# Attention, plan and experts in one program block, expert 0's weights fetched beside the last attention steps, router logits from the unnormalised residual

## The reference

```python
def encode(x, meta_tokens, layers, ln_final_g):
    h = concatenate([meta, x])
    h = h + mixer(rmsnorm(h, p['ln_mix_g']), cos, sin, p)   # windowed attention + gated recurrence, then w_out
    h = h + hier_moe(rmsnorm(h, p['ln_ffn_g']), p)
    return rmsnorm(h, ln_final_g)[:, N_META:]

def hier_moe(u, p):
    grp_logits = uf @ p['w_router_grp'] + p['b_router_grp']      # 4 groups
    grp = argmax(grp_logits)
    exp_logits = uf @ p['w_router_exp'] + p['b_router_exp']      # 32 experts, 8 in each group
    top_v, top_i = lax.top_k(in_grp, TOP_K)                      # the best 2 of the group
    gates = softmax(top_v) * p_grp
    y = expert_dispatch(uf, eid, gates, p['w_exp_gate'], p['w_exp_up'], p['w_exp_down'])

    # for each block of rows of one expert e:
    hid = silu(xb @ w_g[e]) * (xb @ w_u[e])
    return hid @ w_d[e]
```

## Time and profile before

| | us |
|---|---|
| median of 3 runs | 1351.04 |
| lowest and highest of them | 1347.70, 1357.88 |
| the profiled execution | 1343.24 |
| its span in the trace | 1341.2 |
| PE, DVE, ACT, POOL busy | 1203.2, 888.6, 852.0, 281.4 |
| last product of `mix` starts | 602.35 |
| first product of `experts` starts | 654.44 |

### The profile page before, as it was taken

One profiled execution on the slowest core, in us unless ns is written; L12 is line 12 of the kernel. 1 busy time (PEld: TensorE's weight loads), 2 busy tenths in 40 slices (PEclk: granted clock), 3 DMA queues, 4 the chain that ended last, 5 costly groups with the idle time before them and its releaser, 6 DMA issues.

```text
span 1341.2 us, 21877 instructions
## 1 busy us (share of the span) xinstructions
PE 1203.2 (90%) x5939; PEld 1010.3 (75%) x5939; DVE 888.6 (66%) x1111; ACT 852.0 (64%) x1017; POOL 281.4 (21%) x264
## 2 busy tenths in 40 slices
PE   4999999965999999991599999999999999999972
PEld 3998888954778888881378888888888778888851
DVE  5574555343567676653488886565788788888874
ACT  6438888353566665641477775555677677777772
POOL 1000000013022232111013322212232433323320
PEclk9999999955999999995699999999999999999996
DMA  5251110075222224201999988787899999999985
GB/s 188 94 212 40 39 39 16 0 271 156 79 88 83 82 85 132 79 33 35 367 353 388 385 336 296 269 308 265 327 389 380 356 374 377 385 382 380 401 308 234
DMA packets 68710, 302.06 MB, mean 225 GB/s; under 512 B 11883, under 2 KB 22636, under 8 KB 44098
## 3 DMA queue, kind: packets, MB, share of 16 engines
q1 hardware_dynamic: 50850, 262.96, 50.5%
q0 software_dynamic: 17824, 38.66, 11.6%
HBM read 264.57 MB, written 44.43 MB: 230 GB/s over the span
## 4 chain that ended last, share of the span: by engine, by line
PE 35%; DMA 11%; issue 2%; POOL 1%; DVE 1%; POOLq 1%; ACT 1%; ACTq 0%; DVEq 0%; SPq 0%
PE ps_g L1905 11%; PE ps_ey L1942 11%; PE ps_u L1905 10%; DMA h_dram<-y_sb,ix_y 6%; PE ps_ex L1896 2%; DMA ex<-u_dram,ix_x 1%; POOL ix_x L1818 1%; PE ps_eh L1928 1%; DMA late_dram<-y_sb,ix_a 1%; POOLq L1752 1%; DMA z_late<-late_dram,ix_b 1%; DMA out<-cz 0%; DMA raw_d<-in_w_down 0%; DVE g_lo L2067 0%; DVE d_lo L2067 0%
## 5 line engine op out<-in xcount | busy, mean ns | idle before, releaser
L2067 DVE TENSOR_TENSOR d_lo<-raw_d,d_hi 128x2048 fp32r<-128x2048 f32 x62 | 139.5, 2292 | 53.2 <-ACT d_hi L1974 50.8
L2067 DVE TENSOR_TENSOR g_lo<-raw_g,g_hi 128x2048 fp32r<-128x2048 f32 x64 | 143.9, 2289 | 46.3 <-ACT g_hi L1974 46.3
L2067 DVE TENSOR_TENSOR u_lo<-raw_u,u_hi 128x2048 fp32r<-128x2048 f32 x64 | 143.8, 2289 | 10.9 <-ACT u_hi L1974 10.7
L1974 ACT ACTIVATE g_hi<-raw_g 128x2048 fp32r<-128x2048 f32 x64 | 119.2, 1909 | 34.2 <-DMA raw_g<-in_w_gate 25.2
L590 PE MATMUL pj<-h_hi,w_hi 128*128 128x432 f32 x336 | 123.2, 367 | 0.1
L590 PE MATMUL pj<-h_lo,w_hi 128*128 128x432 f32 x336 | 120.5, 359 | 0.0
L590 PE MATMUL pj<-h_hi,w_lo 128*128 128x432 f32 x336 | 120.2, 358 | 0.0
L1974 ACT ACTIVATE u_hi<-raw_u 128x2048 fp32r<-128x2048 f32 x64 | 118.7, 1906 | 0.0
L1905 PE MATMUL ps_g<-g_hi,ex_hi 128*128 128x512 f32 x280 | 112.5, 402 | 5.2 <-DVE ex_lo L2083 5.2
L1974 ACT ACTIVATE d_hi<-raw_d 128x2048 fp32r<-128x2048 f32 x62 | 115.0, 1907 | 0.0
L1905 PE MATMUL ps_u<-u_hi,ex_hi 128*128 128x512 f32 x280 | 113.5, 405 | 0.0
(11 more groups left out here) (292 smaller groups left out, 2696.7 us busy)
## 6 DMA issues: line engine op xcount, KB each, us to landing
raw_g<-in_w_gate SPq DMA_DIRECT2D x64, 1024.0 KB
raw_u<-in_w_up SPq DMA_DIRECT2D x64, 1024.0 KB, 9.8
raw_d<-in_w_down SPq DMA_DIRECT2D x64, 1024.0 KB, 10.7
k_win<-k_dram POOLq DMA_DIRECT2D x20, 384.0 KB, 5.5
w_raw<-in_w_in SPq DMA_DIRECT2D x14, 512.0 KB, 3.9
late_dram<-a_g SPq DMA_DIRECT2D x11, 512.0 KB, 6.5
xh<-in_x SPq DMA_DIRECT2D x10, 512.0 KB, 6.2
h_dram<-xh SPq DMA_DIRECT2D x10, 512.0 KB, 2.7
```

The source lines that it names most:

```text
L1974: act.activation(hi[c][:, :], raw[c][:, :], ACT.Copy).then_inc(hi_done, 1)
L2067: dve.tensor_tensor(lo[c][:, :], raw[c][:, :], hi[c][:, :].bitcast(F32), ALU.subtract).then_inc(lo_done, 1)
```

## The change

1. **One block.** `mix`, `plan` and `experts` write into one `nc.Block()`; the two barriers between them are gone, and each engine walks from one stage into the next. Semaphore waits take the barriers' place: `table_in` before the first use of the table (PE behind `turn_x(1)`, ACT behind `silu_of(0)`, DVE behind the splits of expert 0, SP behind `g_final`, POOL behind `list_y(0)`), `u_out` and `listed` on SP before `lists` is read, `u_out`, `h2_out` and `lists_in` on POOL before the first gather.
2. **Tiles at fixed places.** Since no memory is given back, the tiles of `experts` are laid by address over dead tiles of `mix`: `g_hi`, `g_lo`, `u_hi`, `u_lo` over `wo_hi` and `wo_lo`, the raw gate weights over `q_pre`, the raw up and down weights from the window buffers `k_win` on, and so on. The eight PSUM banks are one tensor `ps`; `square` of the final norm lies in PSUM.
3. **Prefetch.** SP issues expert 0's gate weights in the last attention step (t = 9) and its up and down weights in the next, when the last scores and values are through.
4. **Logits from h.** `turn_u` transposes `xh` itself as soon as `y_read` says that a half is summed. The router is scaled once by `g` (`scale_router`), and `rstd_h` comes in where the bias is added (L1461 of the new program). For the last block, ACT squares behind the two PSUM copies, and DVE writes `u` (`ffn_scale`) behind `hot`; the store of `h2` waits for the sum alone.
5. **Places of single steps.** PE ranks block 8 before its last six output products. The row buffer `xh` is refilled after `turn_u` has read it. POOL takes column 0 of `lists` for the first block without the table. ACT and DVE split all of expert 0's weights at the start, with `split(0, downs)` right behind `x_split(0)`.

```diff
@@ encoder
-            mix(nc, sem, a, (k_pre, v_pre), q_pre, rec, rstd_rec, wo_hi, wo_lo, k_dram, v_tok, v_meta, ident, eps_t, iota_e,
-                counts, h2_dram, u_dram, list_dram)
-        table = top.enter_context(nc.sbuf_tensor("table", [1, MAXBLK * FIELDS], I32))
-        plan(nc, sem, counts, table, table_dram)
-        experts(nc, sem, a, ident, eps_t, table, list_dram, u_dram, h2_dram, late_dram, out)
+            ps = mixer.enter_context(nc.psum_tensor("ps", [P, 8, BANK], F32))
+            block = mixer.enter_context(nc.Block())
+            planned = plan_tensors(nc, mixer, sem, block)
...
@@ mix, sync
+        def prefetch(name, k, c):
+            raw, arrived = raws[name][c], raw_in[name][c]
+            sp.dma_start(raw[:, :], a[name][0].rearrange("(c p k) f -> c p (k f)", p=P, k=k)[c]).then_inc(arrived, 16)
         def outer(b, s):
+            if isinstance(b, int) and b == NB - 1:
+                sp.wait_ge(y_read, 4 * b + 6)
+                sp.dma_start(h2_dram[b * P:b * P + P, :], xh[s][:, :]).then_inc(h2_out, 16)
+                sp.wait_ge(u_done, b + 1)
...
+                if b2 is not None:
+                    sp.wait_ge(u_turned, 2 * b2 + 2)
+                    sp.wait_ge(h2_out, 16 * b2 + 16)
+                    load_x(t, s)
+                if isinstance(t, int) and t == NB - 1:
+                    sp.wait_ge(q_cos_done, NB)
+                    sp.wait_ge(q_swapped, 16 * len(ROTATED) * NB)
+                    for c in range(2):
+                        prefetch("w_gate", 4, c)
+            elif b1 is not None:
+                sp.wait_ge(nmax_done, 2 * NB)
+                sp.wait_ge(av_done, NB + 1)
+                for c in range(2):
+                    prefetch("w_up", 4, c)
+                for c in range(2):
+                    prefetch("w_down", 2, c)
@@ mix, tensor
+            pe.wait_ge(y_read, 4 * b + 5 + i)
...
-                    mm = pe.transpose(ps_t[1 - i][:, k * P:(k + 1) * P], u[:, (4 * i + k) * P:(4 * i + k + 1) * P], ident[:, :])
+                mm = pe.transpose(ps_t[1 - i][:, k * P:(k + 1) * P], xh[s][:, (4 * i + k) * P:(4 * i + k + 1) * P], ident[:, :])
@@ mix, scalar
             if b2 is not None:
                 u_out_of_psum(b2, 1)
+            if last:
+                h2_rms(b2, s)
@@ mix, vector
-                then(dve.tensor_tensor(logits[:, :], ps_x[:, 0:ROUT], rbias[:, :], ALU.add))
+            then(dve.scalar_tensor_tensor(out=logits[:, :], in0=ps_x[:, 0:ROUT], scalar=rstd_h[:, 0:1], in1=rbias[:, :],
+                                          op0=ALU.mult, op1=ALU.add))
...
+            if isinstance(b, int) and b == NB - 1:
+                ffn_scale(b, s)
@@ experts, sync
+        sp.wait_ge(mixed["u_out"], 16 * NB)
+        for s in range(RING):
+            sp.wait_ge(mixed["listed"][s], 16 * NB)
             sp.dma_start(lists[:, :, :], list_dram.rearrange("(p c) o -> p c o", p=P)).then_inc(lists_in, 16)
-            for weights, k, kind in ((a["w_gate"], KG, gates), (a["w_up"], KG, ups), (a["w_down"], KDN, downs)):
-                for c in range(2):
-                    src = weights[0].rearrange("(c p k) f -> c p (k f)", p=P, k=k)[c]
-                    sp.dma_start(kind[0][c][:, :], src).then_inc(kind[3][c], 16)
             sp.dma_start(g_final[:, :], a["ln_final_g"][0].partition_broadcast(P)).then_inc(g_in, 16)
+        sp.wait_ge(table_in, 16)
             load_new(1, a["w_gate"], KG, gates)
@@ experts, scalar
+        act.wait_ge(mixed["y_done"], 4 * NB)
             split(0, gates)
-            x_split(0)
             split(0, ups)
+        act.wait_ge(mixed["u_done"], NB)
+        x_split(0)
+        split(0, downs)
             silu_of(0)
+        act.wait_ge(table_in, 16)
             split_new(1, gates)
             x_split(1)
             split_new(1, ups)
-            split(0, downs)
```

2254 lines of the change are left out of this document (1144 added, 1110 removed).

## The result

The changed kernel took 1337.45 us (median of 20 runs, 1333.3 to 1348.12), the kernel before 1349.02 us (20 runs, 1340.65 to 1357.88) in the same comparison. The ratio of the comparison is 0.9924, with a 95% interval of 0.9905 to 0.9943: 10 us or 0.8% faster (the two medians lie 11.6 us apart). A second comparison gave 0.9928 [0.9900, 0.9955]. The forecast was 15.5 us and 1335.5 us, with a range of 1326 to 1343. Sign and range held. In the profiled executions the gain is smaller: 1334.59 us against 1343.24, with a span of 1332.9 against 1341.2, which is 8.3 us.

A forecast was written before the change was run, and what follows sets the result against it. PE bounds the expert stage; the hole before it is one chain of single steps. Terms 6.2 - 0.9 + 6.8 + 2.1 + 0.8 + 0.5 = 15.5 us, taken from 1351.04, gave 1335.5 us, range 1326 to 1343.

The forecast's parts named there:

- First term: From the last product of `mix` up to the logits' step: that step starts earlier, saving 6.2 us.
- the later of the two branches: Before the logits' step, ACT's square and root end near 607.95, after PE's router product near 607.8.
- Second term: Behind the logits, up to the addresses: DVE writes `u` ahead of four small steps, giving back 0.9 us.
- third term: First barrier, ahead of the plan: the plan starts at once behind `counts`, saving 6.8 us.
- Fourth term: Second barrier, ahead of the lists: table's arrival and barrier no longer hold the lists, saving 2.1 us.
- Fifth term: First gather: 0.8 us saved before POOL's issue, 0.5 us in the gather, taken as 8.2 us instead of 8.66.
- rival A: First gather runs nearly free, about 4 us instead of 8.2, if expert 1's weights come later; 1331.3 us, chance 0.13.
- Prefetch itself: Moving expert 0's six weight transfers beside attention gains 0, since PE waited for the gather.
- The attention steps lose or gain nothing: Attention steps: router's scaling, scaling of `u` and refill of `xh` cost no time; 0 us.
- a stall of PE in the attention steps: Sign in the changed profile that the prediction said would prove it wrong.
- From the first product on: Expert stage from the first gate product: it moves with the gather and itself gains 0.
- Rival D: The shift is given back in the stretch with DMA at 1.00; about 1343 us at worst, chance 0.08.

The follow-up runs named there:

- rlo_late: Changed kernel with POOL's `rec_lo` waiting, from the third step on, until DVE has made `ediff`; 1333.51 us, ratio 0.9901 to the kernel before.
- barriers: Changed kernel cut into three blocks again, so all engines meet between `mix` and `plan` and between `plan` and `experts`; 1342.36 us, ratio 0.9962 to the kernel before.
- best3: Changed kernel plus rlo_late's wait, lists loaded before table, first gather directly from lists, expert 1's weights and `g_final` after it, `ex_lo` before `u_lo`; 1327.07 us.
- stt_before: Kernel before with only the attention steps' logits add exchanged for the change's three-operand form (0.26 us instead of 0.20); 1351.56 us against 1346.40, ratio 1.0042.
- no_prefetch_late: Changed kernel with expert 0's six weight transfers issued behind the lists again and twelve DVE memsets delaying the first scores; 1337.74 us, one profile.
- after_again: The changed kernel itself, measured again as reference for a later group of runs; 1337.67 us, ratio 0.9928 to the kernel before.

## Why the prediction was right or wrong

**First term, 6.2 us: right, 0.6 us short.** The step starts 5.8 us behind the end of the last product instead of 5.2, because the router's product was partly at the low clock (3.05 us; 1.95 in rlo_late, where the stretch gains 6.4 us of the 6.5). The forecast called ACT's root the later of the two branches; in the changed kernel it ends at 614.67 and PE's product decides. The root starts 0.02 us after the load of its function table ends (613.08 + 1.28 = 614.36), so keeping the row, without a further 1.4 us, was right.

**Second term, -0.9 us, and third term, 6.8 us: right.** -0.9 and 6.7 us; barriers confirms the third by putting it back (6.5 us).

**Fourth term, 2.1 us: right in size, wrong in cause.** I called it the second barrier. Of the 2.47 us from the table's load to the lists, the barrier by itself is worth 0.4 us, as barriers shows; the rest, by difference, was the wait for the table to land, which the changed kernel no longer has ahead of the lists.

**Fifth term, 0.8 and 0.5 us: wrong, they are 0.1 and -0.8.** The step that failed is "ACT and DVE now split gate and up weights before the gather lands (9 us of DVE from 619.2 on)". I counted these splits as free, because DVE was idle. They stand beside POOL's copy (1.56 us instead of 0.19) and its issue (2.15 instead of 1.07): 2.4 us of which none was in the sum. best3 takes the splits away from there and has 1.04 us. The gather's size, 8.2 us, was read from one row under other rivals; it is 9.4 us beside 4 MB, counted from an issue that is itself 1.1 us longer, and 4.2 us alone, 1.0 us above the prediction's estimate of 3.2. I had put rival A at 0.13 for the case that expert 1's weights come late by themselves. They did not, since SP issued them at 632.54, ahead of the gather. The mechanism of the rival was right, its condition was not met.

**Prefetch itself, 0: right** in the handover (38.5 us without it, 39.1 with it), but in part by luck: the forecast had neither POOL's 2.4 us beside the early splits nor the 1.7 us by which `ex_lo` is late without them, and the two nearly cancel.

**"The attention steps lose or gain nothing": wrong by 3.4 us** (from the first to the last value product 252.0 us before, 255.4 after). This is the largest miss, and one of the signs that the prediction itself named, a stall of PE in the attention steps (1.09 us in the step shown). I counted the router's scaling, the scaling of `u` and the refill of `xh`, and passed over the logits' own step, since 0.06 us of DVE off the critical path seemed nothing. stt_before shows that in the kernel before this alone makes the three additional long steps; no_prefetch_late shows that it need not, where the steps begin at another distance. It was to be seen: the profile before has one step of 29.2 us with `ediff` at 0.98 us, and `rec_lo` starts within 0.3 us of `ediff` in all others. Rather than ask whether DVE was busy, I should have asked what it holds or is held by.

**The end of mix.** The low clock takes 1.5 us that were in no term, cause open. The ranks of block 8, moved ahead of the last six products, take 21.84 - 21.41 = 0.4 us where I had 0.3. Another 1.6 us are the start of the first step: its value product stands at 328.93 before and 330.54 after, and between 328.8 and 331.8 in the twelve profiles without an added delay, so I take it for scatter.

**From the first product on, 0: not contradicted.** The profiles give 2.3 us of gain there (686.8 us before, 684.5 after, to the end of the span), but the fourteen profiles of this study range from 682.8 to 691.1, and after_again has 688.1. This stage cannot be read from single profiles to better than 4 us. Rival D has no support.

Together: 13.0 us in the handover, less 3.4, 1.5, 0.4 and 1.6, plus 2.3, is 8.4 us, the 8.3 us between the spans within rounding. The ratio of the comparison gives 10 us. The forecast of 15.5 us was the gain of the handover (15.8 in the terms of the table, measured 13.0), taken for that of the kernel. That the time of 1335.5 us came within 2.0 us of the measured one, though 4 to 7 us of the gain were missing, is partly luck: it was worked out from 1351.04 us, the median of three runs, and the kernel before measured 1349.02 in the comparison.

## What to carry to other kernels

Before lengthening or moving a small DVE instruction, look at which POOL instruction it starts next to, in every repetition: where the order of the two is decided by hundredths of a microsecond, fix it with a wait (one wait here, for 3.9 us of the kernel's profile). When a transfer or a barrier goes and an idle engine moves its work into the hole, read the hole again for what that work runs beside; and let bulk loads that nobody needs yet wait for the one transfer that everybody needs (4.1 us here for one line).
